# An encoder layer with a 32-expert mixture on one core: row transposes placed by K halves, moved by ScalarE, and the second norm's gains put on the stored rows

## The reference, cut to what matters

```python
x = x + jnp.concatenate([att, pool], axis=-1) @ w_out[l]
x = x + moe(rmsnorm(x, norm2[l]), w_router[l], b_router[l], w_gate[l], b_gate[l],
            w_up[l], b_up[l], w_down[l], b_down[l])
...
logits = (hf @ w_router + b_router)          # hf: the rows normed with norm2
topv, topi = lax.top_k(logits, TOP_K)        # 4 of 32
gates = jax.nn.softmax(topv, axis=-1)
...                                          # for each expert e and its rows xb = hf[tok]:
g = jnp.minimum(xb @ w_gate[e] + b_gate[e], 7.0)
u = jnp.clip(xb @ w_up[e] + b_up[e], -7.0, 7.0)
act = (u + 1.0) * (g * jax.nn.sigmoid(g * 1.702))
y = (act @ w_down[e] + b_down[e]) * gate     # added to the token's row
```

## Time and profile before

| | |
|---|---|
| median of 3 runs | 2437.32 us (2436.66 to 2440.7) |
| profiled execution | 2440.41 us, span 2438.7 us |
| PE busy / ACT busy / DVE busy | 2235.8 / 467.3 / 757.9 us |
| POOL busy | 508.9 us |
| mean granted PE clock | 0.964 |
| first matmul of the first item | 617.94 us |
| weights read | 128 loads of 2048 KB for gate and up together, 64 for down |

### The profile page before, as it was taken

One profiled execution on the slowest core, in us unless ns is written; L12 is line 12 of the kernel. 1 busy time (PEld: TensorE's weight loads), 2 busy tenths in 40 slices (PEclk: granted clock), 3 DMA queues, 4 the chain that ended last, 5 costly groups with the idle time before them and its releaser, 6 DMA issues.

```text
span 2438.7 us, 29578 instructions
## 1 busy us (share of the span) xinstructions
PE 2235.8 (92%) x9757; PEld 1038.4 (43%) x9758; DVE 757.9 (31%) x2029; ACT 467.3 (19%) x1006; POOL 508.9 (21%) x442
## 2 busy tenths in 40 slices
PE   8999899996689988999999899899999999989994
PEld 4444577554334334334434333334443344344441
DVE  2011888354221223222232322222222312233233
ACT  2000687311010111111111111111101111111112
POOL 1032364212121122121211211221122121222121
PEclk9999999997799989999999899999999999999997
DMA  7000111314266866948868795694889777576754
GB/s 270 13 0 5 65 70 53 137 78 172 81 210 229 326 204 205 335 144 302 324 235 289 244 330 165 219 346 121 332 307 367 265 241 292 173 240 237 275 193 155
DMA packets 149248, 502.81 MB, mean 206 GB/s; under 512 B 10169, under 2 KB 34766, under 8 KB 147630
## 3 DMA queue, kind: packets, MB, share of 16 engines
q1 hardware_dynamic: 113200, 446.79, 47.9%
q0 software_dynamic: 34128, 50.35, 10.2%
q10 hardware_dynamic: 1874, 5.02, 0.5%
HBM read 463.82 MB, written 42.50 MB: 208 GB/s over the span
## 4 chain that ended last, share of the span: by engine, by line
PE 82%; DVE 8%; issue 4%; DMA 2%; ACT 2%; POOL 1%; DVEq 1%; ACTq 0%; POOLq 0%
PE psum L1407 41%; PE psum L1443 14%; PE psum L1184 9%; PE psum L1242 5%; PE psum L1454 3%; PE psum L1343 2%; DVE work L881 2%; PE psum L1401 2%; PE psum L1415 2%; PE psum L1468 1%; DMA weights<-in_w_down 1%; POOL osq L564 1%; DVE work L1115 1%; PE psum L1231 1%; DVE work L1063 1%
## 5 line engine op out<-in xcount | busy, mean ns | idle before, releaser
L1407 PE MATMUL psum<-weights,work 128*128 128x512 f32 (+2 forms) x3520 | 1043.3, 601 | 0.0
L1407 PEld LDWEIGHTS psum<-weights,work 128*128 128x128 f32 (+2 forms) x3520 | 386.6, 154 | 487.3 <-issue 479.9
L1443 PE MATMUL psum<-weights,work 128*128 128x512 f32 x768 | 341.5, 592 | 0.0
L633 POOL DMA_INDIRECT residual_rows<-work x188 | 293.1, 1559 | 229.2 <-ACT work L766 180.1
L601 POOL DMA_INDIRECT work<-normed_rows,work x49 | 49.8, 1015 | 1239.8 <-DVE work L1005 1174.7
L1184 PE MATMUL psum<-weights 128*128 128x512 f32 x512 | 220.5, 593 | 2.6 <-DVE weights L824 2.6
L1014 DVE TENSOR_REDUCE work<-psum 128x8 f32 x48 | 8.8, 184 | 644.0 <-PE psum L1357 644.0
L1443 PEld LDWEIGHTS psum<-weights,work 128*128 128x128 f32 x768 | 142.0, 190 | 152.9 <-issue 149.4
L759 ACT ACTIVATE work<-psum 128x256 f32<-128x256 f32 x188 | 72.2, 384 | 643.8 <-PE psum L1407 643.8
L1115 DVE TENSOR_SCALAR work<-psum 128x256 f32<-128x256 f32 x188 | 79.7, 424 | 318.1 <-ACT work L759 311.3
L761 ACT ACTIVATE work<-psum 128x256 f32<-128x256 f32 x188 | 73.3, 390 | 484.1 <-PE psum L1415 484.1
(11 more groups left out here) (199 smaller groups left out, 1677.6 us busy)
## 6 DMA issues: line engine op xcount, KB each, us to landing
weights<-in_w_gate SPq DMA_DIRECT2D x64, 2048.0 KB, 7.8
weights<-in_w_up SPq DMA_DIRECT2D x64, 2048.0 KB, 12.4
weights<-in_w_down SPq DMA_DIRECT2D x64, 2048.0 KB
x<-in_x SPq DMA_DIRECT2D x16, 512.0 KB, 6.9
weights<-in_w_in SPq DMA_DIRECT2D x8, 1024.0 KB, 15.8
residual_rows<-x SPq DMA_DIRECT2D x9, 512.0 KB, 2.6
normed_rows<-work ACTq DMA_DIRECT2D x9, 512.0 KB, 2.7
bias_rows_repeated<-bias_rows SPq DMA_DIRECT2D x4, 1024.0 KB, 9.6
```

The lines of the kernel that those rows point to most:

```text
L633: pl.indirect_dma_start(acc_d[:, :], bass.IndirectOffsetOnAxis(dest[:, b:b + 1], 0), yrow[:, b * BLK:(b + 1) * BLK], None, compute_op=ALU. ...
L1407: mm = pe.matmul(out.rearrange("p (m n) -> p m n", m=2), xT[:, k, lo:lo + cols], wgu[:, :, k, blk * BLK:(blk + 1) * BLK], start=False, sto ...
L1443: mm = pe.matmul(bank(4 + h), actT[:, k, :], wdn[:, k, h * HALF:(h + 1) * HALF], start=False, stop=(k == DT - 1))
```

## The change

The second norm's gains are put on the rows before they are stored and transposed: `xn = x * rstd * gain2`, one DVE instruction (`norm_rows`), with the 1024 gains loaded to all partitions (`gain2`). The moves out of PSUM behind both transposes (h2T and xT) no longer multiply, and ACT does them. DVE's order per tile becomes `norm_rows(i-1)`, `residual(i)`, `top_k(i-2)`; ACT's is the square of tile i, then the store and the h2T moves of tile i-1, and the square is written to a place of its own. In the loop over items `rows(0)` stands behind the matmuls of the lower half of K, `rows(1)` where `rows(0)` stood. An item begins when the lower half of `xT` is there. ACT does the sigmoid of block b+1 ahead of the move of hidden block b, the first move of `xT` ahead of the first sigmoid and the second ahead of the last hidden move. DVE does `choose` and `row_numbers` right behind the hidden blocks, ahead of the wait for the added rows, and its two register loads at the item's start.

```diff
+        gain2 = Z[:, 5120:6144]
+        junk2 = Z[:, 7424:8448]
...
+            sp.dma_start(gain2, t["norm2"].partition_broadcast(P)).then_inc(s_gain2, 16)
             sp.dma_start(w_r[:, :, :], t["w_router"][0].rearrange("(k p) e -> p k e", p=P)).then_inc(s_small2, 16)
...
             def gather_rows(n):
                 pl.wait_ge(s_idx, n + 1)
+                if not isinstance(n, int) or n > 0:
+                    pl.wait_ge(s_xtp, 2 * n)
...
+            def move_h2T(i):
+                for q in range(2):
+                    n = 2 * i + q
+                    act.wait_ge(s_xnps, n + 1)
+                    if i >= 2:
+                        act.wait_ge(s_rops, i - 1)
+                    act.activation(h2T[:, i % 2, 4 * q:4 * q + 4, :].rearrange("p k c -> p (k c)"), bank(4 + n % 2),
+                                   ACT.Copy).then_inc(s_h2, 1)
+
+            for i in range(TT + 1):
+                if i < TT:
+                    act.wait_ge(s_x1, 2 * i + 2)
+                    if i:
+                        act.wait_ge(s_ss2, i)
+                    act.activation(junk2, xv[:, i, :], ACT.Square, accum_out=sumsq[:, i:i + 1]).then_inc(s_ss2, 1)
+                if i >= 1:
+                    store_rows(i - 1)
+                    move_h2T(i - 1)
...
+            def move_xT(n, q):
+                act.wait_ge(s_xtp, 2 * n + (q + 1))
+                act.activation(xT[:, 4 * q:4 * q + 4, :].rearrange("p k c -> p (k c)"), bank(7),
+                               ACT.Copy).then_inc(s_xT, 1)
...
+                    move_xT(j + 1, 0)
+                    sigmoid(0)
+                    sigmoid(1)
+                    move_hidden(0)
+                    sigmoid(2)
+                    move_hidden(1)
+                    sigmoid(3)
+                    move_hidden(2)
+                    move_xT(j + 1, 1)
+                    move_hidden(3)
...
+            def norm_rows(i):
+                dve.wait_ge(s_rs2, i + 1)
...
+                dve.scalar_tensor_tensor(xn[:, i % 2, :], xv[:, i, :], rstd[:, i:i + 1], gain2, ALU.mult,
+                                         ALU.mult).then_inc(s_xn, 1)
...
+                    dve.wait_ge(s_biased, j + 1)
+                    choose(bass.ds(e1, 1))
+                    dve.wait_ge(s_xtp, 2 * j + 3)
+                    row_numbers(chain, idxb[:, 0:3])
                     dve.wait_ge(s_added, j + 1)
                     chain(dve.tensor_copy(dest, nextitem[:, 0:4]))
                     chain(dve.tensor_copy(dgate, nextitem[:, 4:8]))
                     shift_places(j + 1)
-                    move_xT(j + 1)
-                    row_numbers(chain, idxb[:, 0:3])
-                    dve.wait_ge(s_biased, j + 1)
-                    choose(bass.ds(e1, 1))
...
                 pe.wait_ge(s_chosen, j + 1)
-                pe.wait_ge(s_xT, 2 * j + 2)
+                pe.wait_ge(s_xT, 2 * j + 1)
...
                 spread_index(j + 1)
+                rows(0)
                 pe.wait_ge(s_wk[1], 32 * e + 32)
...
                 if tokens == 32:
                     gate_up_ends(0)
                     next_item()
-                    rows(0)
+                    rows(1)
                     down_bias()
                     hidden(0)
                     down_32(0).then_inc(s_dps, 1)
-                    rows(1)
```

65 lines of the change are left out of this document (23 added, 42 removed).

## The result

The changed kernel takes **2355.02 us** (median of 4 runs, 2354.28 to 2361.54) against 2436.99 for the kernel before beside it (4 runs, 2435.95 to 2440.7): a ratio of 0.966, 95% interval 0.9648 to 0.9671, so 82 us or 3.4% faster. The forecast was 2364, with a range of 2350 to 2396.

A forecast was written before the change was run, and what follows sets the result against it. PE bounds the kernel, losing time to waits for DVE's late moves and `choose` and to half clock behind them. Terms 30 + 27 + 5 - 3 + 8 + 4.8 + 0.9 = 72.7 us off 2437.3 gave about 2364 us, range 2350 to 2396.

The forecast's parts named there:

- the term of -3: Two 32-row items: half clock formerly hidden in the down matmuls would now be paid, 3 us off the gain.
- (3), *where weights are late: Two item groups with late `w_down`: only what follows the landing is gained, 2.6 us and 2.2 us.
- the second group's 2.2: Second late-`w_down` group, at 1368.75: 2.2 us gained behind the landing, its 96- and 64-row item included.
- three other 32-row items: Items with half clock behind them, whose loss of 1.6 us each would go: 5 us gained.
- The gather: Gather of an item's rows, wanted half an item earlier: taken as nothing, bounds 0 and +3 us once.
- rival C: At `rows(0)` the gather holds PE mid-item, half clock behind: 44 us slower, 2481 us; chance 0.04.
- a sign of being wrong: At PE's row transposes (L1343): a wait for a DMA of `normed_rows` would show the forecast wrong.
- A: Clock falls elsewhere and short items keep waits of about 1 us: 2404 us, range 2380 to 2415; chance 0.10.
- B: In short items ACT's table load and move outlast the upper half, delaying the sigmoid: 2410 us; chance 0.03.
- D: `rows(1)` still waits, ACT's queue holding the first move; the stall only moves: 2437 us; chance 0.03.

The follow-up runs named there:

- experiment 9: The changed kernel, with DVE's `norm_rows` of the last tile put ahead of `top_k(5)`: 2352.0 us, ratio 0.9643.
- experiment 1: The changed kernel with PE's old order, ACT's moves at the corresponding places, items beginning when both halves of `xT` are there: 2362.43 us, ratio 0.9686.
- experiment 4: The kernel before with only DVE's order changed: register loads at the item's start; `choose`, moves and `row_numbers` ahead of the added-rows wait: 2385.32 us, ratio 0.977.
- experiment 3: The changed kernel with `row_numbers` and `choose` back behind DVE's added-rows wait, register loads back behind the hidden blocks: 2371.05 us, ratio 0.9711.
- experiment 2: The changed kernel, but DVE instead of ACT does the plain moves of `xT`, at the early places: 2358.47 us, ratio 0.9668.

## Why the prediction was right, and where it fell short

**Right.** The bound, the mechanism and nearly every size. The row transposes' waits for a move went from 51.3 us to 0.7 us. The 64-row items came to 24.74 us (24.8 forecast) and gave 31.3 us (30); 96-row items 8.4 (8); the 32-row items and their followers 26.7 (29). What is missing there lies in the first item, which gave 2.2 us instead of 4.5. Half clock is newly exposed in two items (16.74 and 16.64 us), as the term of -3 had it. That its size came out so close is partly luck, since which and how many items show it varies: three with the thinned load, one with the last tile first, none with PE's old order or with ACT's old order of sigmoids. 94 table loads, hidden with 1.5 us or more to spare. The first item began 1.3 us earlier (0.9 forecast), a difference within what this start varies by (experiment 9); the loss within it stands in the trace: the last transposes began at 578.40 instead of 577.20, 1.2 us later (1.5 forecast), for DVE's rows. Nothing became late for the next item's choice.

**Short by 13.4 us of span, 9 of the median.** The step that failed is (3), *where weights are late*, with 15.9 us instead of 4.8 (the second group's 2.2 in that term is 2.1 when it is counted as the first is). "An earlier PE does not bring them earlier. Only what follows the landing goes" was mis-sized in three places, the first two in the group of 878.57. First, what follows the landing: the sum kept 3.6 us for the 32 down instructions, but their 3.64 in the row was half clock. Rows of before not yet shown, and of after, the same matmuls (windows):

```profile
878.57:882.21 3.64, 3.64 (x33) 1.45 (x34) 0.74 (x2) 0.00 (x0) 0.00 (x0) 0.50 0.00 0
```

```profile
865.33:867.26 1.93, 1.93 (x32) 0.93 (x32) 1.14 (x6) 0.00 (x0) 0.25 (x1) 1.00 0.00 0
```

From the landing to the next item it is now 2.07 us instead of 6.61, so 4.5 gained where 2.6 stood. The same place is worth 3.95 in the other group. PE had waited 2.23 us there instead of 4.70:

```profile
861.17 1.93 PE L1496 MATMUL psum<-weights,work 128*32 128x256 f32 x32 [0.56 <-ACT work L785]
865.33 1.93 PE L1496 MATMUL psum<-weights,work 128*32 128x256 f32 x32 [2.23 <-DMA weights<-in_w_down]
867.40 0.39 PE L1429 MATMUL psum<-work 96*128 96x512 bf16 x1
```

Second, the landing itself: counted from the start of the 96-row item ahead it came after 52.0 us instead of 55.0. PE did not leave the halves of K earlier: counted in the same way, SyncE issued the loads of the two halves at 11.5 and 23.6 us, against 11.6 and 23.1 before, and those of `w_down` at 34.3 instead of 35.4. The transfers themselves ran faster, at 342 instead of 317 GB/s on average over the whole stretch. The gather of rows, which shares the DMA engines, had been issued at 35.7 us, beside `w_down`, and now was at 28.2 us; whether this is the cause was not tested. In the other group the landing came 0.3 us later. Third, the 128-row items behind both groups began at half clock and lost 3.0 and 1.7 us (47.92 and 46.64 against 44.90), which the forecast had counted behind three other 32-row items only. The two kernels with the thinned load say the same from the other side: with no late weights the gain is 84.0 instead of 82 us, so the forecast's reason for leaving these items out was no reason.

**The gather** was taken as nothing, with a bound of +3 us once. PE did wait for it once, by more than that bound, behind the 64-row item, at 1310.14:

```profile
1310.14 0.40 PE L1429 MATMUL psum<-work 96*32 96x512 bf16 x4
1310.36 3.61 PE L1435 MATMUL psum<-weights,work 128*32 128x512 f32 x32
...
1317.81 1.11 PE L1371 MATMUL psum<-ident,work 128*128 128x128 f32 x4 [3.55 <-DMA work<-normed_rows,work]
1320.87 5.49 PE L1435 MATMUL psum<-weights,work 128*32 128x512 f32 x32 [1.95 <-DMA weights<-in_w_up]
...
1332.90 1.93 PE L1496 MATMUL psum<-weights,work 128*32 128x256 f32 x32 [1.64 <-DMA weights<-in_w_down]
```

POOL issued the gather at 1309.83, so 8.0 us passed until PE went on. Behind the 3.55 us the transposes take 1.11 us instead of 0.64 and the matmul block 5.49 instead of 3.64: half clock, 2.3 us, that the forecast had not put there. Yet none of this set the item's length. The upper weights were later still, as the forecast said, and behind all of it PE waited 1.64 us more for `w_down`, whose landing ended the item. The item itself grew, from 23.49 to 24.88 us, because the 64-row item ahead became 5.0 us shorter and the landing did not come earlier. So the sign of rival C, which the forecast had also named as a sign of being wrong, is there in one item of 47, and it cost nothing there that can be seen.

**The rivals.** A (less comes back) did not come: PE's busy time fell by 30 us, and the 128-row items were never so even. B did not come by the table rows above. C showed in the one item just told, without its price. D is refuted by L1371's waits; the kernel with PE's old order shows moreover that even the stall of the old places is small once DVE's order is mended.

**What the forecast had not asked** is which part of the change would do the work. It argued by `rows(0)` and `rows(1)` throughout. Taking their new placement out of the changed kernel costs 6 us (experiment 1), and DVE's new order put alone into the kernel before gives 56 (experiment 4). The placement put alone into the kernel before was not run, so what it would give there is not known. It need not be little: with most of DVE's old order kept, the rest of the change gives some 70 us (experiment 3). The parts remove the same stall, so they overlap and their sizes do not add. The second norm's part is no gain anywhere; it cost 10 us in the kernel before, and what it costs inside the changed kernel was not run apart. It is what lets ACT do the move, and experiment 2 shows that this was not needed for the time.

## What to carry to other kernels

When an engine waits for a small move on another engine, look first at what stands ahead of that move in the other engine's program: here register loads, a wait and three tiny copies made 1.8 of 3.4 us, and moving them out of the way, of the move and of the choice, gave two thirds of the gain. Price a stall with the slow matmuls behind it, and check each duration used as "what is left" against a row at full clock before it is kept in a sum. And an item left out of a sum because another resource bounds it can still gain behind that bound.

## What the runs showed of the hardware

- Half clock is not a function of the stall's length alone. Behind 1.61 us the seven groups of matmuls ran at full speed; behind 3.04 us five of seven were slow, by 0.5 to 1.7 us, two not at all. The Trainium skill (TensorE: Matmul & The Clock Gate, "What's actually happening") says that the number of slow matmuls in one kernel varies from run to run. The rows here show that it also varies from place to place within one run. The kernel with the second norm's part and plain copies has an item at full speed even behind 3.51 us:

```profile
1273.09 0.66 PE L1357 MATMUL psum<-ident,work 128*128 128x128 f32 x4 [3.51 <-DVE work L1077]
1273.67 1.94 PE L1468 MATMUL psum<-weights,work 128*64 128x512 f32 x8
```

- A stretch without late moves is also steadier: 128-row items of the changed kernel lie within 0.1 us of each other but for the two that begin with 9.0 and 5.6 us of issue; before, without these two places, they ranged from 44.85 to 47.93 us.
- A gather of 128 rows takes longer than its own 1 us on POOL by far: 8.0 us from issue to PE's release while weights stream, and leaving out the second half of `w_down` shortened PE's wait only from 3.55 to 3.24 us.
- The pauses called issue at the head of an item (8.9 us before and 9.0 after at the first 128-row item) were untouched by the change and by the thinned weight transfer; with PE's old order the first was 7.6 us. Their cause was not tested. What the trace shows is that packets of 16 KB of the instruction queue moved within them, while no weights did. The changed kernel's queues from 633.83 to 642.80 us (packets, MB, share of the engines):

```profile
q0 software_dynamic: 439, 0.79, 46.9%
q8 instruction: 2, 0.03, 2.5%
```
